# A mixed projection written to HBM in two parts: token-shift mixing moved from a pass over HBM tiles into the projection's PSUM reads

## What is computed

```python
proj = h @ w_in                      # (1024, 3072); columns: attention 1536 | RWKV 1024 | gMLP 512
pb = proj[..., A_COLS:A_COLS + B_COLS]
prev = pad(pb[:, :-1], one zero row on top)
p = pb + (prev - pb) * mu            # mu: one factor for each of the 1024 RWKV columns
```

## Time and profile before

| | us |
|---|---|
| median of 3 runs | 2055.75 |
| lowest and highest run | 2050.84, 2063.43 |
| the profiled execution | 2060.4 |
| its span, as in the trace | 2058.6 |
| `project` in it, to the start of `attend` | 0 to 380.3 |

### The profile page before, as it was taken

One profiled execution on the slowest core, in us unless ns is written; L12 is line 12 of the kernel. 1 busy time (PEld: TensorE's weight loads), 2 busy tenths in 40 slices (PEclk: granted clock), 3 DMA queues, 4 the chain that ended last, 5 costly groups with the idle time before them and its releaser, 6 DMA issues. The chain is left out here.

```text
span 2058.6 us, 34565 instructions
## 1 busy us (share of the span) xinstructions
PE 1834.8 (89%) x9973; PEld 1290.8 (63%) x9974; DVE 1275.9 (62%) x2306; ACT 1001.7 (49%) x1890; POOL 443.5 (22%) x344
## 2 busy tenths in 40 slices
PE   3999998477599788998699999999999999999991
PEld 2778886254488644444367677777677667767761
DVE  6576635588478534344366666666667666666665
ACT  3422210377466422222356666666666566666663
POOL 0000000000022102134123333333333233333331
PEclk9899999799699888999799999999999999999996
DMA  9156315500200192221579989899889999899965
GB/s 352 50 183 219 120 36 175 201 16 18 87 5 11 38 360 83 63 73 43 175 198 321 292 229 310 236 340 335 270 253 326 313 327 282 234 303 328 321 162 183
DMA packets 169083, 405.16 MB, mean 197 GB/s; under 512 B 27060, under 2 KB 39693, under 8 KB 165916
## 3 DMA queue, kind: packets, MB, share of 16 engines
q1 hardware_dynamic: 136284, 300.96, 41.4%
q0 software_dynamic: 32720, 103.16, 20.3%
HBM read 341.65 MB, written 82.13 MB: 206 GB/s over the span
## 5 line engine op out<-in xcount | busy, mean ns | idle before, releaser
L2170 DVE TENSOR_TENSOR w_low<-w_experts,w_high 128x1024 fp32r<-128x1024 f32 x392 | 453.8, 1219 | 137.2 <-ACT w_high L2130 135.6
L2130 ACT CAST w_high<-w_experts 128x1024 fp32r x392 | 382.0, 1046 | 53.5 <-issue 47.8
L2244 PE MATMUL ps_y<-w_experts,actT 128*128 x768 | 346.4, 594 | 5.4 <-issue 5.4
L2221 PE MATMUL ps_h<-w_high,xT_high 128*128 128x512 f32 x776 | 317.2, 409 | 9.2 <-DVE xT_low L2176 9.2
L2221 PE MATMUL ps_h<-w_low,xT_high 128*128 128x512 f32 x776 | 309.1, 398 | 0.0
L2221 PE MATMUL ps_h<-w_high,xT_low 128*128 128x512 f32 x776 | 308.9, 398 | 0.0
L2111 POOL DMA_INDIRECT acc<-y_rows,scatter_idx x96 | 153.9, 1603 | 651.3 <-DVE idx L2163 365.6
L2244 PEld LDWEIGHTS ps_y<-w_experts,actT 128*128 128x128 f32 x768 | 138.8, 191 | 144.5 <-issue 144.2
L2093 POOL DMA_INDIRECT gathered<-h,idx x96 | 169.4, 1765 | 46.4 <-issue 29.0
L2221 PEld LDWEIGHTS ps_h<-w_high,xT_high 128*128 128x128 f32 x776 | 148.1, 191 | 41.7 <-issue 6.7
L2154 ACT COPY y_rows<-ps_y 128x512 f32<-128x512 f32 x96 | 56.4, 588 | 238.8 <-PE ps_y L2244 236.4
(11 more groups left out here) (405 smaller groups left out, 2961.4 us busy)
## 6 DMA issues: line engine op xcount, KB each, us to landing
w_experts<-in_exp_w SPq DMA_DIRECT2D x512, 256.0 KB, 5.8
w_experts<-in_exp_w SPq DMA_DIRECT2D x128, 512.0 KB, 7.2
qT<-in_w_ada POOLq DMA_DIRECT2D x16, 1024.0 KB, 5.4
w_raw<-in_w_in SPq DMA_DIRECT2D x24, 512.0 KB, 7.2
w_ada<-in_w_ada SPq DMA_DIRECT2D x8, 1024.0 KB, 12.1
pb<-pb_tile SPq DMA_DIRECT2D x16, 256.0 KB, 2.6
mix_cur<-pb SPq DMA_DIRECT2D x8, 512.0 KB, 4.3
mixed<-mix_cur SPq DMA_DIRECT2D x8, 512.0 KB, 5.7
```

What stands on the lines that cost most here:

```text
L2130: act.copy(w13_s[par][0][:, which, k], w13[:, bass.ds(w, 1), which, k].squeeze(1)).then_inc(w_high, 1)
L2170: dve.tensor_tensor(w13_s[par][1][:, which, k], w13[:, bass.ds(w, 1), which, k].squeeze(1), w13_s[par][0][:, which, k], ALU.subtract).then ...
L2221: q = pe.matmul(ps_h[:].rearrange("p (a n) -> p a n", a=2), xT[a][:, k, :], w13_s[par][z][:, :, k, :], start=(k == 0 and m == 0), stop=(k ...
L2244: q = pe.matmul(ps_y[n][:], aT[:, k, :], w2[:, bass.ds(w, 1), k, n * BANK:(n + 1) * BANK].squeeze(1), start=(k == 0), stop=(k == FC - 1))
```

## The change

VectorE reads each RWKV unit out of PSUM itself, twice: first the unit times `mu` (the part that belongs to the next token's row), then the unit minus that product (the token's own part). Each unit is so two tiles, `pb_own` (two buffers) and `pb_prev` (three buffers). SP stores the own part into `mixed`; GpSimd then adds the other part to `mixed` one row further down by a transfer that accumulates (`accum_op=ALU.add`). The tiles and `mu` lie in parts of the tensor `v` that are free until group V. The mixing pass at the end, its loads, its stores and the tensor `pb` go.

```diff
@@ sync @@
-            def store_pb(u):
-                sp.wait_ge(proj_read, u + 1)
...
+            def store_own(i):
+                t = i % UNITS
+                sp.wait_ge(pb_read, i + 1)
+                sp.dma_start(dr["mixed"][t * P:(t + 1) * P, mixed_cols(i)], pb_own[i % 2]).then_inc(own_out[i % 2], 16)
...
+            sp.wait_ge(x_mm, 2 * KC)
+            sp.dma_start(mix_mu, io["rwkv_mu"][0:1, :].partition_broadcast(P)).then_inc(mu_in, 16)
...
-                if PB0 * UNITS <= u < (PB1 + 1) * UNITS:
-                    store_pb(u)
+                if PB0 * UNITS < u <= (PB1 + 1) * UNITS:
+                    store_own(u - 1 - PB0 * UNITS)
...
-            def load_tile(t):
...
-            def store_tile(t):
...
@@ gpsimd @@
+            def add_prev(i):
+                t = i % UNITS
+                after = i if t == UNITS - 1 else i + 1
+                for k in (i, after):
+                    pool.wait_ge(own_out[k % 2], 16 * (k // 2 + 1))
+                pool.wait_ge(pb_read, i + 1)
+                n = P - 1 if t == UNITS - 1 else P
+                pool.dma_start(dr["mixed"][t * P + 1:t * P + 1 + n, mixed_cols(i)], pb_prev[i % 3][0:n, :], accum_op=ALU.add).then_inc(prev_out[i % 3], 16)
...
+            for u in range(6 * UNITS):
+                if u in ADA_AT[:-2]:
+                    load_ada(ADA_AT.index(u) + 2)
+                if 0 <= u - 10 < 2 * UNITS:
+                    add_prev(u - 10)
...
@@ scalar @@
             def evacuate(u):
                 g, n = u // UNITS, u % UNITS
+                if g in (PB0, PB1):
+                    return
...
                 elif g == V:
+                    if n == 0:
+                        act.wait_ge(pb_read, 2 * UNITS)
+                    elif n in (2, 3):
+                        act.wait_ge(own_out[n - 2], 16 * UNITS)
+                    elif n in (4, 5, 6):
+                        act.wait_ge(prev_out[n - 4], 16 * len(range(n - 4, 2 * UNITS, 3)))
...
@@ vector @@
+            def mix(u):
+                i = u - PB0 * UNITS
+                own, prev, src = pb_own[i % 2], pb_prev[i % 3], bank[u % RING][:]
+                if i == 0:
+                    dve.wait_ge(mu_in, 16)
+                if i >= 2:
+                    dve.wait_ge(own_out[i % 2], 16 * (i // 2))
+                if i >= 3:
+                    dve.wait_ge(prev_out[i % 3], 16 * (i // 3))
+                dve.wait_ge(proj_mm, u + 1)
+                tt(prev, src, mix_mu[:, mixed_cols(i)], ALU.mult).then_inc(pb_step, 1)
+                dve.wait_ge(pb_step, i + 1)
+                tt(own, src, prev, ALU.subtract).then_inc(pb_read, 1)
+
             for u in range(6 * UNITS):
                 g, n = u // UNITS, u % UNITS
+                if PB0 * UNITS < u <= (PB1 + 1) * UNITS:
+                    mix(u - 1)
                 if n % 2 == 1 and g < 5:
                     low(g + 1, n // 2)
...
-            def mix(t):
...
             for h in range(AH - 1):
                 bias_of(h)
-                mix(h)
...
-            for t in range(AH - 1, NT):
-                mix(t)
@@ tensor @@
                 if u >= RING:
-                    pe.wait_ge(proj_read, u - RING + 1)
+                    old = u - RING
+                    if old // UNITS in (PB0, PB1):
+                        pe.wait_ge(pb_read, old - PB0 * UNITS + 1)
+                    else:
+                        pe.wait_ge(proj_read, old + 1 if old < PB0 * UNITS else old + 1 - 2 * UNITS)
```

More of the change, by code:

```diff
@@ L104, in project @@
         bias_rows = acc[0][:, 0:AH * 3 * P].rearrange("p (h n) -> p h n", h=AH)
-        mix_mu = nc.alloc_sbuf_tensor_at("mix_mu", [P, B_COLS], F32, offset=w_at)
-        mix_cur = [nc.alloc_sbuf_tensor_at(f"mix_cur{j}", [P, B_COLS], F32, offset=w_at + (1 + j) * B_COLS * 4) for j in range(3)]
-        mix_prev = [nc.alloc_sbuf_tensor_at(f"mix_prev{j}", [P, B_COLS], F32, offset=w_at + 2 * KC * BANK * 4 + j * B_COLS * 4) for j in range(3)]
+        v_tile = keep["v"]
+        mix_mu = v_tile[:, 0:2, :].rearrange("p t n -> p (t n)")
+        pb_own, pb_prev = [v_tile[:, 2 + j, :] for j in range(2)], [v_tile[:, 4 + j, :] for j in range(3)]
+        mixed_cols = lambda i: slice(i // UNITS * BANK, (i // UNITS + 1) * BANK)
         stack_in, consts_in = sem("stack_in"), sem("consts_in")
@@ L118, in project @@
         proj_mm, proj_read = sem("proj_mm"), sem("proj_read")
-        pb_out = [sem(f"pb_out{j}") for j in range(2)]
+        pb_step, pb_read, own_out, prev_out = sem("pb_step"), sem("pb_read"), [sem(f"pb_own_out{j}") for j in range(2)], [nc.alloc_semaphore(name=f"pb_prev_out{j}") for j in range(3)]
         wsT_mm, wsT_done = sem("wsT_mm"), sem("wsT_done")
@@ L124, in project @@
         full_ready = sem("h_full_ready")
-        mu_in, mix_in, mix_done, mix_out = sem("mix_mu_in"), [sem(f"mix_in{j}") for j in range(3)], sem("mix_done"), [sem(f"mix_out{j}") for j in range(3)]
+        mu_in = sem("mix_mu_in")
         table_in, table_done, bias_mm, bias_rows_ready, bias_rows_out, bias_in = (sem(n) for n in (
@@ L208, in _ @@
                 sp.dma_start(keep["bias"][:, h, :], src).then_inc(bias_in, 16)
[L209 to L212, removed]
+            for j in range(2):
+                sp.wait_ge(own_out[j], 16 * UNITS)
             sp.wait_ge(yc_out, 16 * NT)
@@ L218, in _, with load_ada @@
         def _(pool):
-            pool.wait_ge(x_mm, KC)
-            for n in range(2 * KC):
+            def load_ada(n):
                 if n >= 2:
@@ L224, in _ @@
                 pool.dma_start(ada_slot[n % 2], io["w_ada"][0][r * P:(r + 1) * P, HALF * (1 + n // KC):HALF * (2 + n // KC)]).then_inc(slot_in[n % 2], 16)
+            def add_prev(i):
[6 more added lines that the diff above has]
+                pool.dma_start(dr["mixed"][t * P + 1:t * P + 1 + n, mixed_cols(i)], pb_prev[i % 3][0:n, :], accum_op=ALU.add).then_inc(prev_out[i % 3], 16)
+            pool.wait_ge(x_mm, KC)
+            load_ada(0)
+            load_ada(1)
+            for u in range(6 * UNITS):
[3 more added lines that the diff above has]
+                    add_prev(u - 10)
+            for j in range(3):
+                pool.wait_ge(prev_out[j], 16 * len(range(j, 2 * UNITS, 3)))
         @block.scalar
@@ L2407, in build @@
             finish(nc, io, dr, keep, out)
-DUMP = ["rows", "pb", "ymix", "x2", "h2", "acc", "out_x"]
+DUMP = ["rows", "mixed", "ymix", "x2", "h2", "acc", "out_x"]
 _INS = ['x', 'c', 'w_ada', 'b_ada', 'norm_pre_mix', 'norm_post_mix', 'norm_pre_ffn', 'norm_post_ffn',
```

26 lines of the change are left out of this document (removed).

## The result

The changed kernel takes 2045.72 us (median of 14 runs, 2034.02 to 2051.75), the kernel before 2055.88 in the same number of runs. The ratio is 0.9942, with a 95% interval of 0.9927 to 0.9957: 0.6% faster, some 12 us, where 20.8 were forecast. The time lies inside the forecast range, in its upper half; the gain is about half of the one forecast.

What follows compares the result with a forecast made beforehand. The mixing pass was taken to bound the end of `project`, TensorE its middle. Savings of 31.1 less a loss of 10.3 gave 20.8 us off: 2055.75 - 20.8 = 2035 us, range 2025 to 2050.

Steps and rivals of the forecast that it cites:

- What bounds the kernel now: In `project`: the mixing pass bounds the end, TensorE the middle, with VectorE not far behind at 71% busy.
- What goes, 31.1 us: Time saved at the end of `project` and the start of `attend`, three terms: 18.4, 11.0 and 1.7 us.
- the tail: From TensorE's last copied unit to the start of `attend`: 18.8 us, of which about 0.4 stays, saving 18.4.
- the stall: In group K between units 42 and 43: idle time and a half-clocked unit, 17.53 - 6.51 = 11.0 us saved.
- the cold matmuls: First 8 matmuls of `attend`, 3.78 us after 19 us of idling; running them warm saves 1.7 us.
- VectorE's new work: In `project`: 16 `mix` of 1.42 us, 22.7 us in all; without waits for adds the chain loses 0.7 us.
- The add behind a load, 7.1 us after the slot: In slots with an adaLN block: 5.4 for the 1 MB load, 0.9 for the add's bytes, 0.8 for adding.
- the slot-by-slot sum: Table of VectorE's slot ends, 9 to 23: last `low` at 213.4 against 203.1 before, so `project` loses 10.3 us.
- The add alone, 4.0 us: GpSimd's adding transfer in a slot without an adaLN block: lands about 4.0 us with its issue.
- Own stores land 2.9 us after their `mix`: SP's 256 KB stores of the own part: each lands 2.9 us after its `mix`.
- adds land late: Rival: adds land 8 to 11 us after a load, alone 5 to 8; loss 14 to 31, 2038 to 2056 us; chance 0.21.
- my own forecast: Middle of `project` loses 4 to 14 us, time 2028 to 2039 us; chance 0.43.

Runs made afterwards that it cites:

- e4: The kernel before without the mixing pass, ScalarE's copies stored unmixed in the tensor `attend` reads: 2023.99 us, ratio 0.9835.
- e1: The changed kernel without its 16 adding transfers and every wait for them, VectorE's products kept: 2029.86 us, ratio 0.9868 to the kernel before.

## Why the prediction came out as it did

**What bounds the kernel now**: held. The end belonged to the mixing pass.

**What goes, 31.1 us**: held, 18.8 less 0.27 for the tail, 11.0 for the stall, 1.8 for the cold matmuls; e4 measured 32.0 as a whole.

**VectorE's new work**: held. The product from PSUM takes 0.69 us in every row, as the row before said; the 65 ns more for a PSUM source by the Trainium skill's rule (VectorE: DVE Perf Modes, the section on the TRN2 errata) do not show in the changed kernel either. Slots 9, 10 and 11 end within 0.1 us of the table, and e1 puts the cost of this work at 1.9 us in the middle, forecast 0.7.

**The add behind a load, 7.1 us after the slot**: too short by about 1, and this is the term of the sum that failed most. Add 0 was waited for until 135.59, 8.2 after the slot's end at 127.38. The parts of that, from the trace: GpSimd's load went out 0.3 after the slot's end and took 5.9 instead of the 5.4 of the median row, and the add landed 1.9 behind it, where I had 0.9 for its bytes and 0.8 for adding. With 8.2 for 7.1, and all else as predicted, the slot-by-slot sum gives a loss of 15 us at unit 24 where it gave 10.3, and the trace shows 17.7 there. The mechanism was the right one and its size was off.

**The add alone, 4.0 us**: held for an add with nothing in its way, of which three landed in 3.9 to 4.0. That is partly luck: a plain transfer of GpSimd's takes 2.3 with its issue, where the working starts from 2.6 and adds the issue, and adding costs 1.6 there and not 0.8, and the two misses cancel. Add 1 had company (an own part's store, then a load) and took 4.7; it went out at 136.20 and freed VectorE at 141.07. The 0.8 was half the difference of two indirect transfers of 512 KB, as if it went by the bytes; right behind a load it is near the 0.9 measured. The rule of the Trainium skill on adding (Collectives: The Full Stack, "The bandwidth ceiling"), two reads and half the rate, is told there of a ring of collectives and was read as 0.9 us for adding. The trace agrees right behind a load (0.9); alone, adding costs more than that (1.6).

**Own stores land 2.9 us after their `mix`**: failed too, and by more in itself. It was a row of the kernel before, taken over for a store that is issued at another moment. The median is 5.3, the first one behind a load and an add took 6.8. Alone it is cheap, since the add stands behind its load for most of that time anyway: with 6.9 instead of 2.9 the sum goes from 10.3 to 11.8, and with the measured adds as well (8.2, and 4.9 for the ones with company) to 16.7, of the 17.7 in the trace. Slot 13 shows the effect: the table has no wait there, the trace 1.81 us, because add 1 could not go out before the own part it overlaps had landed. From there the table runs behind:

| slot | forecast end | trace |
|---|---|---|
| 10 | 127.5 | 127.4 |
| 12 | 138.4 | 139.3 |
| 13 | 144.0 | 146.6 |
| 15 | 160.6 | 162.5 |
| 17 | 176.3 | 181.4 |
| 19 | 188.9 | 195.0 |
| 21 | 201.5 | 209.3 |
| 23, `low` | 213.4 | 221.1 |

7.7 us late at the `low` that releases unit 24, which so ended at 228.8 instead of 221.5. In slot 17 the 5.1 us come over the weights of group 3: SP issues those behind the own part of `mix` 15, at 166.96 instead of 163.6, and their first piece took 6.8 us to ScalarE's rounding (173.78), not 5.15. So a late add costs a second time, through SP's queue. The last 2.1 us were lost in group V, where I had said TensorE keeps its pace: it waited 1.8 us there for a normalisation.

**The rivals**: what happened is the size of "adds land late" (loss 14 to 31, the loss was 19.8), and by its mechanism. The chance I gave the forecast over it rested on the landing of 7.1 us; one more microsecond there is enough to pass from the one to the other, because the chain of three buffers hands every delay on to the next add. So the range held because it took in that rival, while my own forecast (loss 4 to 14, 2028 to 2039) missed. The other half of the cause, a store under load that holds GpSimd back, stood among the things that would prove me wrong, as did a landing outside 6 to 8 us, but without a price. The slowest store of the kernel before, 6.6 us for the one that went out just behind a load, would have been that price.

**Sum**: 31.1 - 19.8 = 11.3; `attend` ends 11.0 us earlier in the trace (517.84, before 528.85), the medians differ by 10.2 and the ratio gives 12.

What stays open: from the end of `attend` to the end of the span the profiled executions take 1529.8 us before, 1526.0 after, and 1521.3 to 1530.1 in the runs above, with no change of code there. Nothing here says why, so a difference of 3 or 4 us between two profiles is not the change's.

## What to carry to other kernels

A transfer's landing time belongs to the moment of its issue and not only to its size: where a change gives the issue to another engine's rhythm, look what that engine releases just ahead of it, and price the store by the landings of the ones that had such company, not by the median. When a freed buffer hangs on a chain of two transfers, count buffers by the whole chain (six instead of three won 15 us of the 19.8), or turn the queue's order (one slot later won 13) before rebuilding anything. Set two profiles to the same moment ahead of the change before comparing times in them: here their starts differed by up to 2.6 us, more than some of the effects. And before removing a slow pass, look at what its first wait is for: here one transfer of 127 partitions made the stall of 11 us, and a cut in two gave back as much as the rebuilding.

## What the runs showed of the hardware

- A load of 127 partitions by 4 KB that SP issued took 26 us to land, at 25 to 27 GB/s and a DMA share of 0.06 to 0.07 (one of 16 engines); the two loads of 128 partitions issued behind it took 18.4 and 18.0. With it cut into 112 and 15 partitions the longest was 9.6. (The adds of 127 partitions that GpSimd issues, in the changed kernel, landed like their neighbours: 8.1 and 6.4 us, each behind a load.)
- Adding into HBM instead of storing costs a 256 KB transfer of GpSimd's 1.6 us when nothing is in its way (3.9 against 2.3) and 0.9 right behind a 1 MB load (medians 7.4 and 6.5); 0.33 of it is its issue on GpSimd (0.872 against 0.539 us).
- A 256 KB store of SP's that lands in 2.0 to 2.5 us with no load near takes 4.9 to 5.3 when a 1 MB load went out 1.2 us before it (e1), and 6.8 to 7.5 with an add between them (the kernel after).
- Behind some nine us of idling the granted TensorE clock was 0.50 (1.2 GHz) in 155 to 160 and back at 1.00 in 165 to 170.
